# First attention of a two-block transformer kernel: TensorE's work of two groups put together in every second step

## The reference

```python
def sliding_window_sink_attention(q, k, v, sinks):
    nb = seq // BLOCK                                  # 4 blocks of 128
    qb = q.reshape(bsz, nb, BLOCK, N_KV_HEADS, GROUP, HEAD_DIM)
    kb, vb = band(k), band(v)                          # the previous block and this one: 256 keys
    s = jnp.einsum('bnqkgd,bnskd->bnkgqs', qb, kb).astype(jnp.float32) * scale
    valid = (dist >= 0)[None] & (dist < WINDOW)[None] & (abs_k >= 0)
    s = jnp.where(valid[None, :, None, None], s + alibi[None, None], -jnp.inf)
    m = jnp.maximum(jnp.max(s, axis=-1, keepdims=True), sink)
    p = jnp.exp(s - m)
    denom = jnp.sum(p, axis=-1, keepdims=True) + jnp.exp(sink - m)
    p = (p / denom).astype(v.dtype)
    return jnp.einsum('bnkgqs,bnskd->bnqkgd', p, vb)
# in the layer:  y = o * silu(gate);  x = x + y @ w_out
```

## Time and profile before

| | |
|---|---|
| median of 3 runs | 1145.09 us (1144.65 to 1145.69) |
| the profiled execution | 1148.06 us, its span 1146.0 us |
| busy share of the span | PE 96%, PEld 82%, DVE 54%, POOL 46%, ACT 38% |
| mean granted clock of TensorE | 0.992 of full speed |
| first attention | 339.0 to 427.5 us of the span, 88.5 us |
| chain that ended last | PE 70%, DVE 9%, issue 8%, POOL 6%, ACT 6%, DMA 1% |

### The profile page before, as it was taken

How to read it: one execution, slowest core, us unless ns; L and a number is a source line. 1 busy time by engine, 2 the same in 40 slices (tenths; PEclk the granted TensorE clock), 3 DMA queues, 4 the chain that set the end, 5 groups by cost and what they waited for, 6 DMA issues and landing times.

```text
span 1146.0 us, 16131 instructions
## 1 busy us (share of the span) xinstructions
PE 1101.0 (96%) x5801; PEld 940.1 (82%) x5801; DVE 619.3 (54%) x1102; ACT 435.5 (38%) x890; POOL 523.6 (46%) x521
## 2 busy tenths in 40 slices
PE   6999999999989999999999887999999999999998
PEld 5788888888869998888798886888878888888887
DVE  6869686668556763656655547856521321321321
ACT  5364758453335661213565578522110200210210
POOL 0000000000352434979833647229956776776772
PEclk9999999999999999999999989999999999999999
DMA  6332322313220101333311200103423222322221
GB/s 251 114 107 76 127 90 95 128 56 113 92 90 19 37 21 36 112 100 122 121 34 50 74 1 20 56 19 111 129 74 105 97 92 94 103 96 92 93 91 53
DMA packets 27279, 97.18 MB, mean 85 GB/s; under 512 B 3024, under 2 KB 3408, under 8 KB 27088
## 3 DMA queue, kind: packets, MB, share of 16 engines
q1 hardware_dynamic: 27216, 96.32, 25.1%
HBM read 94.21 MB, written 2.10 MB: 84 GB/s over the span
## 4 chain that ended last, share of the span: by engine, by line
PE 70%; DVE 9%; issue 8%; POOL 6%; ACT 6%; DMA 1%; POOLq 0%; SPq 0%; DVEq 0%; ACTq 0%
PE bank L1298 20%; PE bank L1300 20%; PE bank L1299 20%; PE bank L805 4%; PE bank L769 3%; POOL wl L1251 3%; PE bank L785 2%; POOL wh L1248 2%; DVE arena L2026 1%; DVE wl L1977 1%; ACT wh L1657 1%; POOL wl L1250 1%; DMA x<-x_in 1%; POOL hold L1247 1%; DVE arena L2361 0%
## 5 line engine op out<-in xcount | busy, mean ns | idle before, releaser
L1247 POOL TENSOR_TENSOR hold<-hold 128x2 f32<-128x2 f32 x117 | 29.9, 256 | 521.4 <-PE bank L1300 521.4
L1298 PE MATMUL bank<-xh,wh 128*128 128x512 f32 x568 | 227.1, 400 | 11.9 <-DVE xl L1946 9.8
L1299 PE MATMUL bank<-xl,wh 128*128 128x512 f32 x568 | 222.7, 392 | 0.0
L1300 PE MATMUL bank<-xh,wl 128*128 128x512 f32 x568 | 222.7, 392 | 0.0
L1298 PE MATMUL bank<-yh,wh 128*128 128x512 f32 x520 | 204.1, 393 | 2.9 <-DVE yl L2366 2.4
L1299 PE MATMUL bank<-yl,wh 128*128 128x512 f32 x520 | 203.0, 390 | 0.0
L1300 PE MATMUL bank<-yh,wl 128*128 128x512 f32 x520 | 203.0, 390 | 0.0
L1251 POOL TENSOR_TENSOR wl<-raw,wh 128x512 fp32r<-128x512 f32 x117 | 173.7, 1484 | 0.0
L1250 POOL TENSOR_TENSOR wl<-raw,wh 128x512 fp32r<-128x512 f32 x117 | 158.5, 1355 | 9.8
L1298 PEld LDWEIGHTS bank<-xh,wh 128*128 128x128 f32 x568 | 107.5, 189 | 35.2 <-issue 12.1
L1300 PEld LDWEIGHTS bank<-xh,wl 128*128 128x128 f32 x568 | 107.6, 189 | 22.8
(11 more groups left out here) (258 smaller groups left out, 1801.0 us busy)
## 6 DMA issues: line engine op xcount, KB each, us to landing
raw<-weight_units SPq DMA_DIRECT2D x173, 512.0 KB, 3.5
x<-x_in SPq DMA_DIRECT2D x4, 512.0 KB, 8.0
out_fm<-x SPq DMA_DIRECT2D x8, 256.0 KB, 2.0
arena<-tables SPq DMA_DIRECT2D x1, 1024.0 KB, 10.3
par<-params SPq DMA_DIRECT2D x1, 166.0 KB, 2.3
arena<-swa_table SPq DMA_DIRECT2D x1, 128.0 KB, 11.1
ident<-identity SPq DMA_DIRECT2D x1, 64.0 KB, 8.3
```

The source lines that it names most:

```text
L1247: pool.tensor_tensor(hold[:], hold[:], hold[:], ALU.add).then_inc(held, 1)
L1298: pe.matmul(out, lh, rh, start=start, stop=False)
L1299: pe.matmul(out, lh, rl, start=False, stop=False)
L1300: return pe.matmul(out, ll, rh, start=False, stop=stop)
```

## The change

TensorE's loop no longer does one group a step in the first attention. A new function `two_groups` does nothing in odd steps; in even steps i it does the scores of groups i+4 and i+5, the transposes of i and i+1, then the values of i-2 and i-1. The pair's transposes, the parts of the items and the tails keep their steps. The lists of DVE, ACT, POOL and SP are unchanged, as are buffers and banks. The second attention (`a == 2`) keeps its order.

```diff
+                def two_groups(i):
+
+                    if i % 2:
+                        return
+                    for do, lag in ((scores, -LOOK - 1), (turn, 0), (values, V_LAG)):
+                        for k in (i - lag, i - lag + 1):
+                            if 0 <= k < ng:
+                                do(k)
+
...
-                    if 0 <= ahead < ng and not late:
+                    if a == 1:
+                        two_groups(i)
+                    elif 0 <= ahead < ng and not late:
                         scores(ahead)
                     if i == -2 and a == 2:
                         behind_scores()
-                    if 0 <= i < ng:
+                    if a == 2 and 0 <= i < ng:
                         turn(i)
-                    if 0 <= i - V_LAG < ng:
+                    if a == 2 and 0 <= i - V_LAG < ng:
                         values(i - V_LAG)
```

## The result

The changed kernel takes 1152.16 us, median of 15 runs (1147.08 to 1156.96), beside 1145.4 us for the kernel before on the same chip (15 runs, 1142.97 to 1148.76). The ratio is 1.0058, 95% interval 1.0042 to 1.0075: slower by 6.7 us, where 4.1 were forecast with 1151.9 as the upper end. Two later comparisons gave 1.0046 (1.0025 to 1.0067) and 1.0051 (1.0033 to 1.0069).

The account below looks back on a forecast made before the run. TensorE and DVE bound the first attention by feeding each other, lead mattering more than work. Waits of 3.3 + 1.1 + 0.3 = 4.7 us, less 0.6 for changeovers, add 4.1 to 1145.09: 1149.2 us, range 1145.6 to 1151.9.

Parts of the forecast that it names:

- S13: Scores of group 13, first stretch of the first attention: a new wait of 0.74 us for DVE's mask of group 10.
- S28: Scores of group 28, behind an item's end in the first attention: a wait of 0.96 us, DVE's `pair_out` taking 1.97.
- S29: Scores of group 29, right behind those of 28: a wait of 1.13 us for DVE's mask of group 26.
- T61: Transposes of group 61, near the end of the first attention: a wait of 0.3 us for ACT's copy of group 59.
- Changeovers, 0.6 us less: TensorE switching between scores, transposes and values: 64 sequences become 32, about 0.02 us saved for each, 0.6 us in all.
- The bound of 2.6 us: Upper bound on the changeover saving: 0.08 us at the first score matmul behind values, 32 times, if that were lost time.
- rival 1: Changeovers are dear: grouping gives 2.6 us against waits of 4.7, 1147.2 us; by the draining rule 3.4 back; chance 0.16.
- a step pair of 18 loads under 2 us: Sign against the forecast: a TensorE step pair of 18 weight loads falling clearly under 2 us in the changed profile.
- The path's sum, 4.1 us: First attention: 4.7 us more TensorE waiting (3.3 + 1.1 + 0.3) less 0.6 for changeovers, net 4.1 us slower.
- rival 3: TensorE's clock falls to 1.2 GHz after standing: one fall more makes 1150.9 us, one fewer 1147.5; chance 0.12 that it decides.
- The delay goes through in full: Output projection and second block follow from the first attention, so its 4.1 us delay was expected whole in the total time.
- Rival 2: DVE gets transposes in twos and keeps a lead through `pair_out`: waits vanish, -3.3 - 0.6, 1141.2 us; chance 0.07.

Follow-up runs that it names:

- scores in twos: Against the kernel before, only the scores of two groups are put together in every second step, transposes and values stay one group a step; ratio 1.0037.

## Why the prediction was right or wrong

- **What bounds the stage, the waits and their places.** Right. S13, S28 and S29, S44 and S45, S60 and S61, T61 wait, the wait before pairs 1, 3 and 5 is gone. S29 was put at 1.13 and took 1.1; S13 at 0.74, took 0.70. S28 was put at 0.96 and took 0.58, because the gating took 0.88, not 1.33. It began 2.55 us behind S24, as forecast; the prediction checked only that POOL would still be splitting then. The rows say that what counts is the rest of POOL's instruction under way: 0.33 us were left and 0.55 followed, where before 0.79 were left. By the rows of before, 373.93 to POOL's next start at 374.21, the cost could have been worked out. By the Trainium skill (SBUF — State Buffer, Who interferes with whom) the second SBUF input of such a DVE instruction comes through a read interface that it shares with GpSimd; the traces agree, 0.88 and 1.33 beside POOL against 0.69 without.
- **Changeovers, 0.6 us less.** Wrong, they give nothing: a pair step of 16 loads is 1.83 against 1.82, and the kernel with transposes and values in twos, which has as few, has 1.0003. The bound of 2.6 us and the drain of rival 1 are refuted with it. The prediction's sign for this, a step pair of 18 loads under 2 us, could not be read: steps in twos have 16 or 17 loads, and its own rows already gave 1.82.
- **The path's sum, 4.1 us.** About right, with some luck, since two errors partly cancel: 3.5 us in the stage of the two profiles. The waits' growth was put at 4.7. From start to start, the falls taken off, the stage grew by 1.0 up to S24 (1.1 forecast), 0.6 and 0.7 from S24 to S40 and to S56 (1.1 each), 1.2 from there with T61's wait (1.4): 1.2 less, nearly all of it the gating. The changeovers' 0.6 was not there to be taken off. All waits for masks and copies are 6.0 us where 8 were forecast.
- **The step that failed: rival 3, the clock, "chance 0.12 that it decides".** Falls were taken as an accident of later places, one more or fewer. They belonged into the sum: the waits that the prediction itself put at 0.96 and 1.13 us side by side bring them, in three of three profiles of the change once each in the first attention behind one of the three places, and 2.3 us in the mean. With 3.8 + 2.3, known only from these runs, the forecast would have been 1151.2. The range ended 0.3 us under the median for the same reason.
- **"The delay goes through in full."** Right by the means, not readable in the pair of profiles, whose spans differ by falls in places the change does not touch. The prediction named "the stage is 4 us longer and the span is not" as a sign against it, and that pair shows it (3.5 longer, span 0.9 shorter). It was a bad sign: it took for granted that the clock falls alike in both executions, the same step that failed above.
- **Rival 2, DVE gets ahead.** Refuted: it stands for the pair's transposes and has the same queue behind them.

What stays open: how much of the spread within the change (0.986 to 0.996) lies in the first attention. No profile of a run at 0.986 was taken. Each profile shows one fall behind the long waits there, worth 1.6 us; the 2.3 us of the mean, and some runs above all, need more than that. And that the falls come from the two close waits is shown by few places: five falls in twelve places with both waits (the change and scores in twos), none in nine where one was shortened or filled.

## What to carry to other kernels

In a pipeline between engines, count for each consumer how much work lies between what feeds it and what waits for it, in the new order; batching equal instructions shortens that for every second one, and here it bought nothing. If they are batched all the same, choose which two: the odd scores paired with the even ones that follow cost 0.3 us of the stage at most here, paired with the even ones of their own step 3.5 us. A TensorE wait of half a microsecond costs itself; several close together can cost the clock too, so add that before calling it a rival. Where runs of one kernel differ by their granted clock, compare stretches at full clock and the means of many runs, never two spans.

## What the runs showed of the hardware

- Going between split float32 products (128x256), transposes and float32 values costs no measurable time: 1.83 us for 16 loads in one step of two groups, 1.82 in two steps of one.
- TensorE standing for DVE by 0.58 and then 1.1 us, one score between them, was followed by 3.4 us at 1.2 GHz in one of three places in each of three profiles; in the kernel with scores in twos by the same at two of three places; with 0.4 and 1.1 (one profile), or with the second wait filled (two), by none in nine such places. The same standing did not bring it each time.
- Work that nobody reads, put into a wait, made the kernel faster: 1147.8 against 1150.1 us in the mean of 12 runs each (difference 0.6 to 3.9, 95%).
- A DVE instruction with two SBUF inputs (128x512) that starts beside POOL's splitting ended 0.54 or 0.55 us behind the POOL instruction under way: 1.33 us with 0.78 or 0.79 left of it, 0.88 with 0.33 left, 0.69 with POOL not splitting.
